# Expert weights in 1 MB transfers: the gate/up slots of a mixture-of-experts loop filled and given back by halves

## The chip, the cores and the metric

One NeuronCore of a Trainium2 chip runs the whole kernel. The metric is the device time of one execution in microseconds (us). The kernel before took 1300.48 us, the median of three executions (1299.77 to 1305.3). The profile is of one further execution, which took 1301.27 us; its traced span, from the first to the last instruction, is 1299.4 us.

## The reference, cut to what matters

One decoder layer over 256 tokens of width 1024, all in float32: three attention-like branches are merged into the residual stream, and then a mixture of experts adds its share. Only the second part matters here. Each token picks 4 of 32 experts; an expert is a product with a 1024 x 2048 matrix (gate and up columns interleaved), a clamped SwiGLU, and a product with a 1024 x 1024 matrix.

```python
def expert_block(args):
    rows, wts, e = args
    hgu = tok[rows] @ w_gu[e] + b_gu[e]
    gate = jnp.minimum(hgu[:, 0::2], SWIGLU_LIMIT)
    up = jnp.clip(hgu[:, 1::2], -SWIGLU_LIMIT, SWIGLU_LIMIT)
    act = (up + 1.0) * (gate * jax.nn.sigmoid(SWIGLU_ALPHA * gate))
    y = act @ w_down[e] + b_down[e]
    return y.astype(jnp.float32) * wts[:, None]
```

The weights of the 32 experts are 32 x 12 MB, and each is read from HBM once. They are the largest part of the 455.63 MB that the kernel moves.

## The kernel before, in words

**Trunk.** Up to about 375 us the three branches run, with their weights in a ring of six 2 MB slots. At the end of this stretch the router's choice is turned into a list of items. An item is one expert with up to 32 of its tokens; this input gives 46 items, and a popular expert has several, which stand one behind the other. Two items make a pair.

**Slots.** One expert's weights are six chunks of 2 MB: chunks 0 to 3 are gate/up weights (`w_gu`), chunks 4 and 5 are down weights (`w_down`). In SBUF there are twelve slots of 2 MB, six for experts on even seats and six for those on odd seats (`slot_no`). Chunk q of `w_gu` holds the weight rows 8p + 2q and 8p + 2q + 1 on partition p, which lie one behind the other in HBM, 16 KB in all. A chunk of `w_down` holds on each partition two stretches of 8 KB that lie apart in HBM. Each slot has a semaphore `w_full`, which the transfer raises by 16 when all of it has landed.

**SyncE (SP)** issues every weight transfer, in one fixed order. Experts 0 and 1 are loaded while the trunk runs (`load_chunk` called directly). In the loop, `load_round` serves one expert after the other: it waits until TensorE has used chunk q of the expert's last item (L505, `gu_done`), and then loads chunk q of the expert after the next into that slot (L394). Behind chunk 1 it waits for `brow_used` (L508) and loads the four 2 KB pieces of the gate/up bias row (L510). Chunks 4 and 5 follow, behind waits for `down_done` (L513). All of this stands in one instruction stream, so that a wait holds up everything behind it. There are 30 such rounds.

**TensorE (PE)** runs over the pairs. `up(q, ...)` (L1094) waits in `landed` (L1083) for the whole chunk q and multiplies it by the tokens, as 2 halves c = 0, 1 of four products each (each recorded as two matmuls, so 16 for a chunk), and its last matmul raises `gu_done` by one. `up(0)` waits for the bias row too. `bias` is L1073, `down` L1119, the gather of tokens L1045, the scatter of results L1053, the turning of activations L1104. The order for one pair is: gather, the first item's chunk 0 and bias, the down product of the item before, the first item's chunks 1 to 3, scatter, the second item's chunk 0 and bias, the first item's down product, the second item's chunks 1 to 3.

**VectorE (DVE)** waits for the item's fourth `gu_done` (L1850) and applies the clamps (L1853 and after). ScalarE (ACT) applies the sigmoid and evacuates the results (L1410 to L1423).

Of the kernel before, what the change touches and what calls it, by code (L numbers as in the profile page):

```python
# [30 lines left out]
P = 128  # L31
# [160 lines left out]
def hybrid_layer(nc, A, const, out):  # L192

    with ExitStack() as ctx:
# [5 lines left out]
        def S(name):  # L200
            if name not in sems:
                sems[name] = ctx.enter_context(nc.semaphore(name))
            return sems[name]
# [19 lines left out]
        slot = [mem[:, a:a + SLOT] for a in slots_at]  # L223
# [18 lines left out]
        w_full = [S(f"w_full{i}") for i in range(NSLOTS)]  # L242

        def C(name):
            a, n = CPART[name]
            return late[:, a:a + n] if a < LATE else cst[:, a - LATE:a - LATE + n]
# [132 lines left out]
        w_gu, b_gu, w_dn = A["w_gu"][0], A["b_gu"][0], A["w_down"][0]  # L379
# [3 lines left out]
        def slot_no(q, odd):  # L383

            return q if not odd else NSLOT + q if q < 4 else 6 + q

        def load_chunk(sp, e, q, odd):

            if q < 4:
                n, src = 2, w_gu[e].rearrange("(p c) n -> p c n", p=P)[:, 2 * q:2 * q + 2, :]  # L390
            else:
                n, src = 2, w_dn[e].rearrange("(c p two) n -> p c (two n)", p=P, two=2)[:, 2 * (q - 4):2 * (q - 4) + 2, :]
            n_slot = slot_no(q, odd)
            sp.dma_start(slot[n_slot].rearrange("p (c n) -> p c n", c=n), src).then_inc(w_full[n_slot], 16)  # L394


        def lines(a):
# [14 lines left out]
        def _(sp):  # L412
            for i in range(NT):
                sp.dma_start(memn[:, i, :], A["mem"][0][P * i:P * i + P, :]).then_inc(mem_in[i], 16)
            def cols(a, c0, n=512):
                return a[:, c0:c0 + n].rearrange("(c p) n -> p c n", p=P)

            src = {
                "mk": cols(w_mkv, 0), "mv": cols(w_mkv, 512), "mq": cols(w_in, C_MQ),
                "qk0": cols(w_in, 0), "qk1": cols(w_in, 512), "v": cols(w_in, C_V), "o": cols(w_in, C_O),  # L420
                "nq": cols(w_in, C_NQ), "nkv": cols(w_in, C_NKV), "kcvc": cols(w_in, C_KCVC, 256),
                "w1k": A["cmp_w1_k"][0].rearrange("(m l) d f -> (l d) m f", l=2),
                "w1v": A["cmp_w1_v"][0].rearrange("(m l) d f -> (l d) m f", l=2),
                "wbm": cols(A["w_br_mem"][0], 0, D), "wbl": cols(A["w_br_ml"][0], 0, D),
                "wbn": cols(A["w_br_nsa"][0], 0, D),
                "wo0": cols(A["w_out"][0], 0), "wo1": cols(A["w_out"][0], 512),
# [73 lines left out]
            def load_round(n, odd):  # L500

                f = sp.value_load(idx[0:1, bass.ds(n, 1)], min_val=0, max_val=ITEMS - 1)
                ahead = sp.value_load(idx[0:1, bass.ds(n + (AT_ORDER + 1), 1)], min_val=0, max_val=NE - 1)
                for q in range(4):
                    sp.wait_ge(S("gu_done"), f * 4 + (q + 1))  # L505
                    load_chunk(sp, ahead, q, not odd)
                    if q == 1:
                        sp.wait_ge(S("brow_used"), f + 1)  # L508
                        for m in range(4):
                            sp.dma_start(brow[not odd][32 * m:32 * m + 1, :],  # L510
                                         b_gu[bass.ds(ahead, 1), 512 * m:512 * m + 512]).then_inc(brow_in[not odd], 16)
                for q in (4, 5):
                    sp.wait_ge(S("down_done"), f * 2 + (q - 3))  # L513
                    load_chunk(sp, ahead, q, not odd)
# [41 lines left out]
        def _(pe):  # L556
# [50 lines left out]
            for half in range(2):  # L607
# [6 lines left out]
                for k in range(4 * half, 4 * half + 4):  # L614
                    for i in range(NT):
                        mm = nc.tensor.matmul(both[i][:, :], memT[:, k, P * i:P * i + P], w[:, k, :],
                                              start=k == 0, stop=k == KT - 1)
# [15 lines left out]
            for n in range(4):  # L633
                w = slot3(f"qk{n // 2}", KT, 512)
                b = begin(f"qk{n}")
                for j in range(2):
                    c0 = 256 * (n % 2) + P * j
                    for k in range(KT):
                        mm = nc.tensor.matmul(b[:, 256 * j:256 * j + 256], w[:, k, c0:c0 + P], uT[:, k, :],  # L639
                                              start=k == 0, stop=k == KT - 1)  # L640
# [7 lines left out]
            for k in range(KT):  # L648
                g = k % 4
                mm = nc.tensor.matmul(b[32 * g:32 * g + 32, 0:SEQ], wgw[:, k, :], uT[:, k, :], start=k < 4, stop=k >= 4)  # L650
# [6 lines left out]
            for j in range(2):  # L657
                mm = nc.tensor.matmul(b[0:4, 256 * j:256 * j + 256], C("sum4")[:, 4 * j:4 * j + 4], gws, start=True, stop=True)
# [39 lines left out]
            for i in range(NT):  # L698
                mm = nc.tensor.matmul(b[:, 24 * i:24 * i + 24], gws[:, P * i:P * i + P], C("sum4")[:, 8:32], start=True, stop=True)
# [57 lines left out]
            for j in range(2):  # L757
                for k in range(KT):
                    mm = nc.tensor.matmul(b[:, 256 * j:256 * j + 256], w[:, k, P * j:P * j + P], uT[:, k, :],
                                          start=k == 0, stop=k == KT - 1)  # L760
# [7 lines left out]
            for n, (name, job) in enumerate((("w1k", "hk"), ("w1v", "hv"))):  # L768
# [4 lines left out]
                for m in range(4):  # L773
                    for g in range(4):
                        mm = nc.tensor.matmul(b[32 * g:32 * g + 32, 0:CMP_HID], blk[:, n, 4 * m + g, :],
                                              w[:, 4 * m + g, :], start=m == 0, stop=m == 3)
                done(mm, job)
            bgate("bgl", 0, 0)
            for n, job in enumerate(("hk", "hv")):
                was_read(pe, job)  # L780
                b = begin(job + "T")
                for f in range(2):
                    mm = nc.tensor.matmul(b[:, 32 * f:32 * f + 32], hidp[:, n, P * f:P * f + P], C("sum4"), start=True, stop=True)
# [9 lines left out]
            for f in range(2):  # L793
                mm = nc.tensor.matmul(b[0:30, 0:DH], hid[:, 0, f, :], w2[:, 0, f, :], start=f == 0, stop=f == 1)
# [3 lines left out]
            for g in range(2):  # L798
                for f in range(2):
                    mm = nc.tensor.matmul(b[0:NCMP, DH * g:DH * g + DH], hid[:, 1, f, NCMP * g:NCMP * g + NCMP],  # L800
                                          w2[:, 1, f, :], start=f == 0, stop=f == 1)
# [104 lines left out]
            for hh in range(2):  # L906
                for j in range(2):
                    job = f"pn{hh}{j}"
                    b = begin(job)
                    for u in range(2):  # L910
                        c0 = 512 * hh + 256 * j + P * u
                        for k in range(4):
                            was_read(pe, f"nv{k}")
                            mm = nc.tensor.matmul(b[:, 256 * u:256 * u + 256], w[:, k, c0:c0 + P], hT_nsa[k],  # L914
                                                  start=k == 0, stop=k == 3)
# [28 lines left out]
            for k in range(KT):  # L944
# [3 lines left out]
                mm = nc.tensor.matmul(b[32 * g:32 * g + 32, 0:SEQ], wr[:, k, :], uT[:, k, :], start=k < 4, stop=k >= 4)  # L948
# [3 lines left out]
            for i in range(NT):  # L952
                mm = nc.tensor.matmul(b[:, NE * i:NE * i + NE], lTs[:, P * i:P * i + P], C("sum4"), start=True, stop=True)
# [33 lines left out]
            for i in range(NT):  # L987
                mm = nc.tensor.matmul(b[0:NE, 33:34], sel[:, i, :], ones[:, 0:1], start=i == 0, stop=i == NT - 1)
# [30 lines left out]
            mm = nc.tensor.matmul(b[0:1, 3 * ITEMS:3 * ITEMS + NE], C("pcol")[0:NE, :], Hs, start=True, stop=True)  # L1019
# [57 lines left out]
            def trunk_turns(n_slot):  # L1077
                return TRUNK_TURNS[n_slot] if n_slot < NSLOT else 0

            def landed(q, e, odd):  # L1080

                n_slot = slot_no(q, odd)
                pe.wait_ge(w_full[n_slot], e * 8 + (8 if odd else 16 * (trunk_turns(n_slot) + 1)))  # L1083
                return slot[n_slot]

            def up(q, e, n, odd):

                if q == 0:
                    pe.wait_ge(brow_in[odd], e * 32 + (32 if odd else 64))
                w = landed(q, e, odd).rearrange("p (c n) -> p c n", c=2)  # L1090
                for c in range(2):
                    k = 2 * q + c
                    for s in range(4):
                        mm = nc.tensor.matmul(BH[n][32 * s:32 * s + 32, :], xgT[:, k, 32 * n:32 * n + 32],  # L1094
                                              w[:, c, 512 * s:512 * s + 512], start=k == 0, stop=k == KT - 1,
                                              skip_group_check=True)
                mm.then_inc(S("gu_done"), 1)

            def turn(i, n, j):

# [347 lines left out]
        def _(dve):  # L1448
# [79 lines left out]
            for n in range(2):  # L1528
                dve.wait_ge(S("conv_sig"), n + 1)
                q = qk[:, 4 * n:4 * n + 4, :].rearrange("p j t -> p (j t)")  # L1530
# [55 lines left out]
            for i in range(NT):  # L1586
                was_read(dve, f"nq{i}")
                q = nq_sb[:, i, :].rearrange("p (h e) -> p h e", h=QH)
# [47 lines left out]
            for n in range(2):  # L1636
                for g in range(2):
                    src = k2[:, n, g, :]
                    src = bass.AP(src.tensor, src.offset, [list(src.ap[0]), [2, 16], [16, NCMP]])
# [207 lines left out]
            step(V.tensor_copy(idx[0:1, AT_PACK:AT_PACK + PAIRS], packed), "idx_ready")  # L1847
            def activate(i, n):

                dve.wait_ge(S("gu_done"), i * 4 + 4)  # L1850
                h = BH[n][:, :].rearrange("p (f two) -> p f two", two=2)
                g, u = gt, ut
                V.tensor_scalar(g, h[:, :, 0], LIMIT, None, ALU.min).then_inc(S("g_clip"), 1)  # L1853
                V.tensor_scalar(u, h[:, :, 1], -LIMIT, LIMIT, ALU.max, ALU.min).then_inc(S("u_clip"), 1)
                dve.wait_ge(S("g_sig"), i + 1)
                V.tensor_tensor(g, g, sg, ALU.mult).then_inc(S("gs_done"), 1)
                dve.wait_ge(S("u_clip"), i + 1)
                dve.wait_ge(S("gs_done"), i + 1)
                V.scalar_tensor_tensor(out=u, in0=u, scalar=1.0, in1=g, op0=ALU.add, op1=ALU.mult).then_inc(S("act_ready"), 1)
# [52 lines left out]
```

## Time and profile before

| What | Value |
|---|---|
| Median of three executions | 1300.48 us |
| The profiled execution | 1301.27 us |
| Its span | 1299.4 us |
| PE busy | 1119.9 us (86%) |
| DVE, ACT busy | 269.4 us, 217.2 us |
| Data moved | 455.63 MB, mean 351 GB/s |

Busy times are summed over the span and say little of what sets the end: they are averages over a trunk and a loop with different limits. The page cuts the span into 40 slices of 32.5 us with a busy digit for each engine (9 is 90% or more), and beneath them the share of time in which the 16 DMA engines were busy and the GB/s that they moved. A DMA share can come out slightly above 1, since the records of packets overlap. "SPq" is SyncE's sequencer, which issues transfers and is never counted as busy.

### The profile page before, as it was taken

What the parts mean: (1) busy time and instruction counts of PE and PEld (TensorE: products, weight loads), DVE (VectorE), ACT (ScalarE), POOL (GpSimd) and SP (SyncE); (2) the same over time, 40 slices, a digit from 0 to 9 for tenths busy, and PEclk for the clock granted to TensorE, in tenths of its full rate; (3) what the DMA queues carried; (4) which work ended last, traced back from release to release, by engine and by line L of the source; (5) the groups of instructions that cost most, each with busy time, mean ns of one, the idle gap of its engine ahead of it and who ended that gap; (6) DMA issues with size and microseconds to landing.
All of it is one profiled execution on the core that took longest, in us unless ns stands there. A gap on an engine that the chain in (4) does not pass through costs nothing.

```text
span 1299.4 us, 19302 instructions
## 1 busy us (share of the span) xinstructions
PE 1119.9 (86%) x7511; PEld 536.1 (41%) x7512; DVE 269.4 (21%) x728; ACT 217.2 (17%) x486; POOL 17.4 (1%) x24
## 2 busy tenths in 40 slices
PE   8999999999999996569976965899597969799957
PEld 4665767888553332123322321333222323243312
DVE  3234424363231111001111100011111101111101
ACT  2115422254021110001100100111010101011101
POOL 1100101000000000000000000000000000000000
PEclk9999999999999998779987977899888979899978
DMA  9942237343679999999999999979999999999996
GB/s 335 356 136 91 91 131 270 123 167 138 262 294 422 423 427 425 427 425 425 426 425 429 425 427 426 426 294 428 426 427 427 424 425 425 428 427 427 425 425 263
DMA packets 66886, 455.63 MB, mean 351 GB/s; under 512 B 7588, under 2 KB 13576, under 8 KB 34088
## 3 DMA queue, kind: packets, MB, share of 16 engines
q1 hardware_dynamic: 66344, 454.48, 85.3%
q10 hardware_dynamic: 448, 0.60, 0.1%
q8 instruction: 21, 0.34, 0.1%
q0 software_dynamic: 64, 0.13, 0.0%
q14 instruction: 9, 0.07, 0.0%
HBM read 454.15 MB, written 1.05 MB: 350 GB/s over the span
## 4 chain that ended last, share of the span: by engine, by line
PE 66%; DMA 23%; SPq 8%; issue 1%; DVE 1%; ACT 1%; ACTq 0%; DVEq 0%
DMA mq<-in_b_gu 22%; PE bank L1094 18%; PE bank L1119 10%; PE bank L590 6%; PE bank L730 6%; SPq L394 4%; PE bank L1045 4%; PE bank L1053 3%; PE bank L1073 3%; SPq L510 3%; PE bank L639 2%; PE bank L926 2%; PE bank L892 2%; PE bank L579 1%; PE bank L914 1%
## 5 line engine op out<-in xcount | busy, mean ns | idle before, releaser
L1094 PE MATMUL bank<-mem 128*32 128x512 f32 x2944 | 359.2, 630 | 156.7 <-DMA mq<-in_b_gu 156.4
L1094 PEld LDWEIGHTS bank<-mem 128*32 128x32 f32 x2944 | 94.7, 114 | 366.9 <-issue 364.2
L1119 PE MATMUL bank<-mem 128*32 128x512 f32 x1472 | 173.0, 611 | 0.7 <-ACT mem L1415 0.7
L1853 DVE TENSOR_SCALAR mem<-bank 128x256 f32<-128x256 f32 x46 | 19.5, 424 | 742.6 <-PE bank L1094 742.6
L1421 ACT ACTIVATE mq<-bank 64x512 f32<-64x512 f32 x46 | 27.1, 590 | 463.0 <-PE bank L1119 463.0
L1119 PEld LDWEIGHTS bank<-mem 128*32 128x32 f32 x1472 | 44.2, 112 | 129.4 <-issue 128.7
L1045 PEld LDWEIGHTS bank<-mem,sc 128*128 128x128 f32 x736 | 83.9, 192 | 19.2 <-issue 19.2
L1045 PE MATMUL bank<-mem,sc 128*128 128x64 f32 x736 | 87.1, 277 | 0.0
L590 PE MATMUL bank<-mem 128*128 128x512 f32 x192 | 83.2, 592 | 0.0
L1053 PE MATMUL bank<-mq,mem 128*128 128x512 f32 x176 | 81.4, 605 | 0.0
L730 PE MATMUL bank<-mem 128*128 128x256 f32 x320 | 71.3, 381 | 0.0
L730 PEld LDWEIGHTS bank<-mem 128*128 128x128 f32 x320 | 60.0, 190 | 8.7 <-issue 0.7
L590 PEld LDWEIGHTS bank<-mem 128*128 128x128 f32 x192 | 36.3, 190 | 43.6 <-issue 43.5
L1410 ACT ACTIVATE mem<-mem 128x256 f32<-128x256 f32 x46 | 19.2, 417 | 208.6 <-DVE mem L1853 208.6
L1073 PE MATMUL bank<-mq,mem 1*32 1x512 f32 x368 | 52.7, 644 | 0.0
L1053 PEld LDWEIGHTS bank<-mq,mem 128*128 128x128 f32 x176 | 31.6, 189 | 50.0 <-issue 50.0
L1415 ACT ACTIVATE mem<-bank 128x256 f32<-128x256 f32 x46 | 17.6, 383 | 141.2 <-PE bank L1108 74.4
L892 PE MATMUL bank<-mem 128*128 128x256 f32 x128 | 28.7, 380 | 0.0
L1073 PEld LDWEIGHTS bank<-mq,mem 1*32 1x32 f32 x368 | 7.4, 109 | 50.3 <-issue 50.3
L579 PE MATMUL bank<-mem 128*128 128x128 f32 (+4 forms) x150 | 20.3, 275 | 8.7 <-DMA mem<-shape_consts 5.8
L926 PE MATMUL bank<-mem 128*128 128x512 f32 x64 | 27.8, 592 | 0.0
L639 PE MATMUL bank<-mem 128*128 128x256 f32 x128 | 27.8, 379 | 0.0
(306 smaller groups left out, 794.5 us busy)
## 6 DMA issues: line engine op xcount, KB each, us to landing
mem<-in_w_gu SPq DMA_DIRECT2D x128, 2048.0 KB, 32.7
mem<-in_w_down SPq DMA_DIRECT2D x64, 2048.0 KB, 37.1
mem<-in_w_in SPq DMA_DIRECT2D x13, 2048.0 KB, 10.5
mem<-in_w_out SPq DMA_DIRECT2D x2, 2048.0 KB, 8.4
mem<-in_w_mem_kv SPq DMA_DIRECT2D x2, 1024.0 KB, 7.1
mem<-in_w_mem_kv SPq DMA_DIRECT2D x1, 2048.0 KB, 8.3
mem<-in_cmp_w_k SPq DMA_DIRECT2D x1, 2048.0 KB, 8.5
mem<-in_cmp_w_v SPq DMA_DIRECT2D x1, 2048.0 KB, 8.1
```

Source lines behind the costliest of these rows:

```text
L394: sp.dma_start(slot[n_slot].rearrange("p (c n) -> p c n", c=n), src).then_inc(w_full[n_slot], 16)
L510: sp.dma_start(brow[not odd][32 * m:32 * m + 1, :], b_gu[bass.ds(ahead, 1), 512 * m:512 * m + 512]).then_inc(brow_in[not odd], 16)
L590: mm = nc.tensor.matmul(b[:, 0:n], src[k][:, P * i:P * i + P], w[:, k, c0:c0 + n], start=k == 0, stop=k == kt - 1)
L639: mm = nc.tensor.matmul(b[:, 256 * j:256 * j + 256], w[:, k, c0:c0 + P], uT[:, k, :], start=k == 0, stop=k == KT - 1)
L730: mm = nc.tensor.matmul(b[:, 256 * j:256 * j + 256], w[:, k, c0 + P * j:c0 + P * j + P], src[k], start=k == 0, stop=k == kt - 1)
L892: mm = nc.tensor.matmul(b[:, 256 * half:256 * half + 256], w[:, k, c0:c0 + P], uT[:, k, :], start=k == 0, stop=k == KT - 1)
L926: mm = nc.tensor.matmul(b[:, :], mg[k][:, P * i:P * i + P], w[:, k, :], start=k == 0, stop=k == KT - 1)
L1045: mm = nc.tensor.matmul(b[:, 64 * c:64 * c + 64], x2[:, t, o:o + P], Gm[:, t].rearrange("p g n -> p (g n)"), start=t == 0, stop=t == NT - 1)
L1053: mm = nc.tensor.matmul(ACC[t][hh][:, :], STs[:, P * t:P * t + P], y_sb[:, 512 * hh:512 * hh + 512], start=False, stop=False, skip_group_c ...
L1073: mm = nc.tensor.matmul(BH[n][p:p + 32, :], ones[p:p + 1, 0:32], brow[row][p:p + 1, :], start=False, stop=False, skip_group_check=True)
L1094: mm = nc.tensor.matmul(BH[n][32 * s:32 * s + 32, :], xgT[:, k, 32 * n:32 * n + 32], w[:, c, 512 * s:512 * s + 512], start=k == 0, stop=k ...
L1119: mm = nc.tensor.matmul(BG[64 * hh + 32 * two:64 * hh + 32 * two + 32, :], actT[:, o:o + 32], w[:, 2 * c + two, 512 * hh:512 * hh + 512], ...
```

## The change

Three things are altered together. `load_chunk` fetches a gate/up chunk by two transfers of 1 MB instead of one of 2 MB: half c is the weight row 8p + 2q + c of each partition, 8 KB. In the loop each half has a wait of its own. TensorE raises `gu_done` after each half of a chunk rather than after the chunk, so that all counts of `gu_done` double (SP's, and VectorE's L1850), and the count of `w_full` for a gate/up slot goes up by 32 for each chunk. TensorE still waits for both halves before it starts a chunk. The down chunks keep their single 2 MB transfers.

```diff
-        def load_chunk(sp, e, q, odd):
+        def load_chunk(sp, e, q, odd, halves=range(2)):
+            n_slot = slot_no(q, odd)
             if q < 4:
-                n, src = 2, w_gu[e].rearrange("(p c) n -> p c n", p=P)[:, 2 * q:2 * q + 2, :]
+                src = w_gu[e].rearrange("(p c) n -> p c n", p=P)
+                for c in halves:
+                    sp.dma_start(slot[n_slot][:, 2048 * c:2048 * c + 2048].unsqueeze(1),
+                                 src[:, 2 * q + c:2 * q + c + 1, :]).then_inc(w_full[n_slot], 16)
             else:
-                n, src = 2, w_dn[e].rearrange("(c p two) n -> p c (two n)", p=P, two=2)[:, 2 * (q - 4):2 * (q - 4) + 2, :]
-            n_slot = slot_no(q, odd)
-            sp.dma_start(slot[n_slot].rearrange("p (c n) -> p c n", c=n), src).then_inc(w_full[n_slot], 16)
+                src = w_dn[e].rearrange("(c p two) n -> p c (two n)", p=P, two=2)[:, 2 * (q - 4):2 * (q - 4) + 2, :]
+                sp.dma_start(slot[n_slot].rearrange("p (c n) -> p c n", c=2), src).then_inc(w_full[n_slot], 16)
...
                 for q in range(4):
-                    sp.wait_ge(S("gu_done"), f * 4 + (q + 1))
-                    load_chunk(sp, ahead, q, not odd)
+                    for c in range(2):
+                        sp.wait_ge(S("gu_done"), f * 8 + (2 * q + c + 1))
+                        load_chunk(sp, ahead, q, not odd, (c,))
...
-                pe.wait_ge(w_full[n_slot], e * 8 + (8 if odd else 16 * (trunk_turns(n_slot) + 1)))
+                n = 32 if q < 4 else 16
+                pe.wait_ge(w_full[n_slot], e * (n // 2) + (n // 2 if odd else 16 * trunk_turns(n_slot) + n))
...
-                mm.then_inc(S("gu_done"), 1)
+                    mm.then_inc(S("gu_done"), 1)
...
-                dve.wait_ge(S("gu_done"), i * 4 + 4)
+                dve.wait_ge(S("gu_done"), i * 8 + 8)
```

## Rows read from the trace of the kernel before

**Rows 1.** The page's slices: PE busy tenths, DMA busy tenths, GB/s, packet counts.

```profile
PE   8999999999999996569976965899597969799957
DMA  9942237343679999999999999979999999999996
GB/s 335 356 136 91 91 131 270 123 167 138 262 294 422 423 427 425 427 425 425 426 425 429 425 427 426 426 294 428 426 427 427 424 425 425 428 427 427 425 425 263
DMA packets 66886, 455.63 MB, mean 351 GB/s; under 512 B 7588, under 2 KB 13576, under 8 KB 34088
```

**Rows 2.** Who waited for whom: engine line <- releaser: us, times, longest.

```profile
PE bank L1094 <- DMA mq<-in_b_gu: 156.4, 14, 13.5
```

**Rows 3.** The chain that ended last: start us, us, what; two items' period repeats.

```profile
668.36 28.89 DMA mq<-in_b_gu
...
728.15 28.87 DMA mq<-in_b_gu
...
787.93 28.88 DMA mq<-in_b_gu
```

**Rows 4.** Timeline of PE, 816 to 882 us: start us, us, instructions merged.

```profile
816.93 3.64 PE L1094 MATMUL bank<-mem 128*32 128x512 f32 x16 [12.75 <-DMA mq<-in_b_gu]
...
865.89 1.93 PE L1094 MATMUL bank<-mem 128*32 128x512 f32 x16
867.74 1.06 PE L1073 MATMUL bank<-mq,mem 1*32 1x512 f32 x8
868.74 3.64 PE L1119 MATMUL bank<-mem 128*32 128x512 f32 x32
872.19 5.33 PE L1094 MATMUL bank<-mem 128*32 128x512 f32 x48
877.46 3.70 PE L1053 MATMUL bank<-mq,mem 128*128 128x512 f32 x8
```

**Rows 5.** Timeline of SP's issues, same columns, from 823 us on.

```profile
823.89 6.63 SPq L394 DMA_DIRECT2D mem<-in_w_down  x2
868.02 6.62 SPq L394 DMA_DIRECT2D mem<-in_w_gu  x2
874.89 1.53 SPq L510 DMA_DIRECT2D mq<-in_b_gu  x4
876.66 1.42 SPq L394 DMA_DIRECT2D mem<-in_w_gu  x2
886.28 2.10 SPq L394 DMA_DIRECT2D mem<-in_w_down  x2
890.17 0.95 SPq L394 DMA_DIRECT2D mem<-in_w_gu  x2
```

**Rows 6.** Stretches: us, engines' busy (instructions), PE clock, DMA share, GB/s.

```profile
25.00:30.00 5.00, 5.00 (x16) 2.40 (x15) 3.62 (x9) 0.32 (x1) 1.02 (x1) 1.00 1.05 398
35.00:40.00 5.00, 5.00 (x13) 2.19 (x12) 0.00 (x0) 0.69 (x1) 0.00 (x0) 1.00 1.05 387
55.00:60.00 5.00, 5.00 (x25) 4.41 (x24) 2.52 (x6) 0.04 (x1) 2.32 (x3) 1.00 1.05 387
860.00:865.00 5.00, 5.00 (x50) 3.58 (x38) 2.03 (x5) 0.42 (x1) 0.00 (x0) 1.00 0.22 90
865.00:870.00 5.00, 5.00 (x45) 1.71 (x47) 0.62 (x2) 0.66 (x2) 0.00 (x0) 1.00 0.33 51
870.00:875.00 5.00, 5.00 (x52) 1.56 (x48) 0.00 (x0) 1.18 (x2) 0.00 (x0) 1.00 0.90 367
```

**Rows 7.** Page's transfers: count, KB each, median us from issue to landing.

```profile
mem<-in_w_gu SPq DMA_DIRECT2D x128, 2048.0 KB, 32.7
mem<-in_w_down SPq DMA_DIRECT2D x64, 2048.0 KB, 37.1
mem<-in_w_in SPq DMA_DIRECT2D x13, 2048.0 KB, 10.5
```

**Rows 8.** Line L394's own instructions on SP: count, ns min/median/max, first and last start.

```profile
L394 SPq FUSED_REGOPS  x180: 37/37/43, 385.5 to 1249.1; - x180
```

## The prediction, made before the changed kernel ran

> **What bounds the kernel now.** I read the 40 slices first. From slice 13 to slice 39 the DMA engines are busy nine tenths or more, but for one slice, and move 422 to 429 GB/s, while PE's digit falls to 5 to 7 again and again [rows 1]. Next the waits: PE stood still before L1094 for 156.4 us in 14 waits, at most 13.5 us, all ended by a transfer landing [rows 2]. In the chain that ended last, such a landing returns with an even beat: 668.36, 728.15, 787.93, so 59.8 us for two experts or 24 MB [rows 3]. Issue to landing takes 32.7 us in the median for gate/up [rows 7], while the twelve chunks of two experts take 59.8 us, 4.98 each: the queue is 32.7 / 4.98, over six chunks, deep. So in the loop the DMA engines set the pace, and PE has some 12 us to spare in most pairs. What the change does is worth what it does to those engines: to their idle time, and to their time per byte.
>
> Idle time of the DMA engines in the loop is found in one place. The slice at 294 GB/s holds it, and narrower stretches show 90 GB/s in 860 to 865, 51 in 865 to 870 and 367 in 870 to 875 [rows 1, 6]. There PE works without a break from 816.93 on items of one popular expert; SP has issued all it may by about 830.5 (823.89 + 6.63), and the next slot comes free only when chunk 0 is used by that expert's last item, at 865.89 + 1.93; SP issues at 868.02 [rows 4, 5].
>
> **The parts of the change.**
>
> Finer release, the gain. In the drained stretch the first 1 MB can be asked for after 8 of the 16 matmuls of 1.93 us, so 0.9 us earlier [rows 4]. Behind it, chunk 1's release comes some 6.2 us after chunk 0's (two issues begin and end within 868.02 + 6.62, and the last takes under 0.5) [rows 5], while a 2 MB chunk needs 4.98 us of the engines; here too the first half may go 0.9 us earlier, which fills a small second bubble. The engines' restart moves by the 0.9 us; both bubbles together could give at most 2 x 0.9 = 1.8 us. I take -0.9. Everywhere else the queue holds chunks enough that asking earlier only means waiting longer in it: nothing.
>
> PE's landing wait still wants both halves, so nothing starts earlier on the far side of the transfer. The end of the kernel hangs on down chunks, which are not split.
>
> Smaller packets, the cost. The page counts 66886 packets, 34088 of them under 8 KB [rows 1]. The difference, 32798, is 128 x 128 (one packet of 16 KB on each partition for each gate/up chunk) plus 64 x 256 (two of 8 KB for each down chunk), which is 32768, plus 30 others. So gate/up goes in 16 KB packets now, and the halves make them 8 KB: on each of the 16 engines a gate/up chunk becomes 16 packets instead of 8.
>
> What does a packet cost beyond its bytes? Two rows fix it. In the trunk the engines are full with 2 KB packets (w_in, 512 columns of float32): 387 GB/s in two stretches and 398 in a third [rows 6]. At 387, a 2 KB packet takes one engine 16 x 2048 / 387e3 = 0.0847 us. Call y the time of 2 KB and k the cost per packet: y + k = 0.0847. In the loop, an engine moves in 59.785 us (the mean beat) 24 MB / 16 = 768 times 2 KB in 64 + 64 = 128 packets, and the engine that carries the bias rows (one packet each, 8 in two experts) has 8 packets of 2 KB more: 768 y + 128 k + 8 (y + k) = 59.785 [rows 3]. This gives 640 y = 48.27, y = 0.0754 us, k = 9.3 ns. At 398 GB/s instead it gives y + k = 0.0823 and k = 6.4 ns. I take 9.3, which two of the three stretches give.
>
> Eight further packets cost a gate/up chunk 8 x 9.3 = 74 ns (51 ns at the low end). The loop loads 30 x 4 = 120 of these chunks. Some lie between the landing that lets PE go at 816.93 and the drained stretch, whose end PE sets; they only shorten the idle time. In those 49 us (to 866) the engines move 49 / 4.98 = 10 chunks, of which two thirds, 6, are gate/up. 114 x 0.074 = +8.5 us; low end 114 x 0.051 = +5.9. The eight chunks loaded in the trunk are fetched one or two at a time as slots come free, beside PE's trunk work; were all of them on the path, it would be 8 x 0.074 = 0.6 us. I take nothing.
>
> One more completion for each chunk on each engine. The trace doesn't price it apart. From below it is nothing (a gain is excluded: work is only added); from above one small packet, k, as the nearest row: 114 x 9.3 ns = 1.1 us. In the beat above the 8 bias transfers fit without a price for their completions; I take the middle, +0.5.
>
> SP: per round four more waits, each with one register operation of 37 ns [rows 8], and four more issues. Two issues end 0.95 us after the first began [rows 5], about 0.5 us each; I take 0.6 with the wait around it: 4 x 0.6 = 2.4 us in a round of 29.9 us. Queued behind them are the bias rows, the down chunks and the next round; the depth of the DMA queue hides it. In the drained stretch that cover is gone, but there the two halves come free 0.9 us apart, longer than the 0.6 us of an issue. Without any cover it would be 30 x 2.4 = 72 us, which the depth excludes. An issue that finds the queue full holds SP up already (6.63 us for two [rows 5]); that costs nothing as long as the queue is what is full.
>
> PE: one more increment per chunk and item, 184 in all. Three chunks run in one piece, 872.19 to 877.46, 0.110 us a matmul with two increments inside; one chunk takes 1.85 for 16, 0.116 [rows 4]. No cost is seen, and there are 12 us of slack per pair. DVE's wait only has another number.
>
> **Sum**: -0.9 + 8.5 + 0.5 = +8.1 us. The profiled span should go from 1299.4 to 1307.5 and its execution from 1301.27 to 1309.4; against the median of the runs shown, 1300.48 + 8.1 = 1308.6 us. The bounds of this case are 5.9 + 0 - 1.8 = +4.1 and 8.5 + 1.1 = +9.6 with no gain at all: 1304.6 to 1310.1.
>
> **What the Trainium skill says of it.** The page "DMA: Bandwidth & Descriptors", section "Bandwidth" (its part on why small descriptors are slow), gives a fixed overhead of about 3 cycles for each packet, and the same section an 850 MHz fabric; that would be 3.5 ns instead of 9.3, by estimate 114 x 8 x 3.5 ns = 3.2 us instead of 8.5. By that rule the sum would be +2.8 us, 1303.3. The same page's fit charges each transfer a fixed 2 us beside its bytes, which would add 2 us for each of the 120 further transfers; it would give a 2 MB chunk 6.8 us where the trace has 4.98 in a deep queue, so the fixed part is hidden here, and I don't count it.
>
> **Rivals.**
>
> Not slower: a packet costs next to nothing, and the lower rate in the trunk belongs to w_in's narrow columns, not to packets. Then the change is the -0.9 us of the drained stretch and the time 1299.6; if a packet costs about a third of my figure it is 114 x 8 x 3.1 ns = 2.8, less 0.9, +1.9: 1302.4. It decides from k below (6.5 + 0.9 - 0.5) / (114 x 8) = 7.6 ns on: there the slowdown falls under 0.5%. For it: the trunk stretches are short and 398 GB/s is among them. Against it: with k = 0 the beat gives y = 59.785 / 776 = 0.0770 us, and 2 KB packets would then run at 16 x 2048 / 77.0 = 425 GB/s; the trunk shows 387 to 398 with the engines full. The 3 cycles of the Trainium skill's page "DMA: Bandwidth & Descriptors", section "Bandwidth", would end near this case's upper value.
>
> Much slower: a cost per transfer, not per packet. If all of the 128 x 9.3 = 1190 ns that I lay on packets in two experts belonged to their 12 large transfers, each would cost 99 ns, and the change adds 114 of them: +11.3 - 0.9 = +10.4, 1310.9. If both exist, 8.5 + 11.3 - 0.9 = +18.9, 1319.4. The same range stands for 8 KB pieces at a 64 KB stride being read less well than the down chunks' 8 KB pieces, which lie close together. Against it: w_in's transfers are of 2 MB as well [rows 7] and yet run slower.
>
> Faster by over 6.5 us: the drained stretch would have to go altogether. The missing bytes there, (425 - 90 + 425 - 51 + 425 - 367) x 5 us, are 3.8 MB or 9 us of the full rate, but no half is free before 0.9 us ahead of today's release.
>
> **How the numbers follow.** The forecast case, a cost per packet of 6.4 to 9.3 ns, 0.64; little or no cost per packet (1299.6 to 1302.4), 0.18; cost per transfer or a worse stride (1310.9 to 1319.4), 0.15; faster, 0.03. The range 1302.0 to 1313.0 takes in the forecast's bounds, the upper end of the second case and the lower part of the third. A measurement of this kernel can tell about 0.5%, 6.5 us, from no change, so above 1307.0 counts as slower: the third case and, of the first, the part near 9.3 ns, some 0.46 of its 0.64. Slower 0.61, within 0.5% 0.36, faster 0.03.
>
> **What the profile of the changed kernel would show.** 66886 + 16384 packets, and with them 128 x 16 = 2048 tiny completions, so about 85,300, of which some 36,100 under 8 KB. The beat of two experts at 59.79 + 8 x 0.074 = 60.4 us, and the full slices at 420 to 423 GB/s instead of 425 to 427. The issue after the drained stretch 0.9 us earlier after PE's chunk began than today's 2.1 us. If the queue counts packets, issue to landing falls for gate/up from 32.7 us to some 20 to 25, at no cost; that would not be a sign of speed. I am wrong if the beat stays at 59.8 (no packet cost), if it exceeds 60.8 (a cost per transfer), or if the DMA share shows new dips, which would mean that the shorter queue runs dry.

## The result and the profile after

The changed kernel takes 1309.26 us in the median of 14 runs (1305.63 to 1311.44), the kernel before 1300.25 us in 14 (1298.87 to 1308.0). The ratio is 1.0059 with a 95% interval of 1.0044 to 1.0073, so it is slower by 5.7 to 9.5 us. The profiled execution of the changed kernel has a span of 1306.9 us, 7.5 more than before.

The page's slices of the changed kernel, as in [rows 1]:

```profile
DMA  9932337334589999999999999979999999999995
GB/s 339 348 134 92 115 134 266 126 138 173 225 335 419 420 421 423 422 422 422 422 421 422 422 422 421 422 319 423 422 421 422 422 422 422 422 421 422 422 422 242
DMA packets 85319, 455.64 MB, mean 349 GB/s; under 512 B 9636, under 2 KB 15624, under 8 KB 36136
```

The same bytes go in 18433 packets more: 16384 data packets and 2048 completions, with one over. The full slices stand at 419 to 423 GB/s, where they stood at 422 to 429. DMA is as busy as before; it is busy for longer with each byte. The drained slice (the 27th) has 319 GB/s instead of 294.

The chain that ended last, changed kernel (start us, us, what), against [rows 3]:

```profile
983.13 21.39 DMA mq<-in_b_gu
...
1043.53 21.40 DMA mq<-in_b_gu
...
1103.91 21.38 DMA mq<-in_b_gu
```

(1103.91 - 983.13) / 2 = 60.39 us for two experts. Before it was 59.785. That is the whole change in one line: +0.60 us for every 24 MB. The waits of PE for a landing are as they were [rows 2]:

```profile
PE bank L1099 <- DMA mq<-in_b_gu: 157.7, 14, 13.3
```

And the page's transfers, against [rows 7] (KB each, median us from issue to landing):

```profile
mem<-in_w_gu SPq DMA_DIRECT2D x256, 1024.0 KB, 24.7
mem<-in_w_down SPq DMA_DIRECT2D x64, 2048.0 KB, 27.9
```

From issue to landing a transfer now takes 8 to 9 us less, and the kernel is slower. For gate/up a part of this is only that a transfer is half as large: in the first run below, with 2 MB transfers of 8 KB packets, it is 29.0 us. A down transfer is as large as before and takes 27.9 us instead of 37.1. So an issue-to-landing time in a full queue does not tell the speed; it tells how much is queued ahead.

The drained stretch, changed kernel: first PE, then SP's issues, then the stretches in which the engines run dry, as in [rows 4 to 6].

```profile
819.54 3.64 PE L1099 MATMUL bank<-mem 128*32 128x512 f32 x16 [12.93 <-DMA mq<-in_b_gu]
...
868.50 1.92 PE L1099 MATMUL bank<-mem 128*32 128x512 f32 x16
```

```profile
869.76 7.46 SPq L393 DMA_DIRECT2D mem<-in_w_gu  x4
877.47 1.54 SPq L514 DMA_DIRECT2D mq<-in_b_gu  x4
879.25 2.45 SPq L393 DMA_DIRECT2D mem<-in_w_gu  x4
```

```profile
865.00:870.00 5.00, 5.00 (x48) 3.74 (x47) 2.08 (x6) 0.96 (x3) 0.00 (x0) 1.00 0.05 21
870.00:875.00 5.00, 5.00 (x48) 1.35 (x48) 0.00 (x0) 0.00 (x0) 0.00 (x0) 1.00 0.85 316
```

SP asks for the first half 869.76 - 868.50 = 1.26 us after TensorE begins that chunk; before, the whole chunk was asked for after 868.02 - 865.89 = 2.13 us. The finer release works, by 0.87 us, in the one place of the loop where the engines wait for it.

### The profile page after: what moved, and what is told of

It is laid out like the page before. It is cut to its first block, busy times and chain, and to the rows that moved or that the text cites. A ratio compares the mean times of both kernels' runs of the same rounds, so it can differ in the third digit from the quotient of the medians.

```text
span 1306.9 us, 19790 instructions
## 1 busy us (share of the span) xinstructions
PE 1126.2 (86%) x7511; PEld 536.1 (41%) x7512; DVE 269.7 (21%) x728; ACT 217.0 (17%) x486; POOL 17.4 (1%) x24
## 4 chain that ended last, share of the span: by engine, by line
PE 60%; SPq 20%; DMA 15%; issue 3%; DVE 1%; ACT 1%; ACTq 0%; DVEq 0%
PE bank L1099 15%; DMA mq<-in_b_gu 15%; SPq L393 11%; PE bank L1124 8%; PE bank L594 6%; PE bank L734 6%; SPq L397 5%; SPq L514 4%; PE bank L1057 3%; PE bank L1049 3%; PE bank L1077 3%; PE bank L643 2%; PE bank L930 2%; PE bank L896 2%; PE bank L583 1%
## 5 line engine op out<-in xcount | busy, mean ns | idle before, releaser
L1099 PE MATMUL bank<-mem 128*32 128x512 f32 x2944 | 359.2, 630 | 158.4 <-DMA mq<-in_b_gu 157.7
## 6 DMA issues: line engine op xcount, KB each, us to landing
mem<-in_w_gu SPq DMA_DIRECT2D x256, 1024.0 KB, 24.7
mem<-in_w_down SPq DMA_DIRECT2D x64, 2048.0 KB, 27.9
```

## The experiments

Three explanations of the 0.60 us a beat were on the table: a cost for each packet (the prediction's), a cost for each transfer, and a cost of the added waits and increments. The first four runs take them apart; the last three turn to what else loads the DMA engines. "Beat" is the time of two experts in the steady part of the loop, read from the chain as above.

**The packets alone.** One transfer of 2 MB and one release, but of two rows that lie apart in HBM.

```diff
-                n, src = 2, w_gu[e].rearrange("(p c) n -> p c n", p=P)[:, 2 * q:2 * q + 2, :]
+                n, src = 2, w_gu[e].rearrange("(p c q) n -> p c q n", p=P, q=4)[:, :, q, :]
```

(The gathered tokens and the gains are put in the matching order: an access pattern of x2 at L1401 and of gcol at L1865.)

> A gate/up chunk stays one transfer of 2 MB with one wait and one release, but holds the weight rows 8p + q and 8p + q + 4, which lie apart in HBM, so its packets are of 8 KB as in the changed kernel. Theory (a cost for each packet, 9.3 ns): the beat of two experts goes from 59.79 to 60.4 us as in the changed kernel, some 83,300 packets, and the time to about 1309 us, +9 against before, without the 0.9 us that the halves win. Rival 1 (a cost for each transfer): the number of transfers is unchanged, so beat 59.8 and 1300 us. Rival 2 (the waits and issues added on SyncE cost): none is added here, so 1300 us too.

Measured: 1312.09 us, ratio 1.0088 (1.0072 to 1.0105); span 1307.8. Its packets and the chain that ended last:

```profile
DMA packets 83270, 455.63 MB, mean 348 GB/s; under 512 B 7588, under 2 KB 13576, under 8 KB 34088
```

```profile
678.72 22.01 DMA mq<-in_b_gu
...
799.46 22.01 DMA mq<-in_b_gu
```

Four experts in 120.74 us, 60.37 a beat. No transfer, wait or increment was added, and the whole slowdown is there. The median is 3 us above the 1309 expected, and the interval of the ratio, +9.4 to +13.7 us, begins a little above +9; why this kernel is slower than its beat asks for is open. The profile is of one of its faster executions (1309.79 us); its span, 1307.8, is 0.9 above that of the changed kernel, the size of the release that this kernel lacks, but one profile each can't show that this is the reason. This run leaves one rival: its packets, too, are read at a stride of 64 KB. The fourth run has no such stride.

**The halves without the finer release.**

```diff
-                    for c in range(2):
-                        sp.wait_ge(S("gu_done"), f * 8 + (2 * q + c + 1))
-                        load_chunk(sp, ahead, q, not odd, (c,))
+                    sp.wait_ge(S("gu_done"), f * 4 + (q + 1))
+                    load_chunk(sp, ahead, q, not odd)
...
-                    mm.then_inc(S("gu_done"), 1)
+                mm.then_inc(S("gu_done"), 1)
...
-                dve.wait_ge(S("gu_done"), i * 8 + 8)
+                dve.wait_ge(S("gu_done"), i * 4 + 4)
```

> The changed kernel with its two transfers of 1 MB for a gate/up chunk, but both issued behind one wait for the whole chunk, and gu_done raised once for a chunk as before. Theory: beat 60.4 us as in the changed kernel, and the issue after the drained stretch comes some 2.1 us after TensorE's chunk began, as before, rather than 1.26 us: 1310 us, 0.9 more than the changed kernel. Rival (the release in halves is what costs, by the waits on SyncE or the increments on TensorE): beat back at 59.8, 1300 to 1302 us.

Measured: 1309.82 us, ratio 1.0074 (1.0058 to 1.009); span 1306.7. The chain, then PE around the drained stretch:

```profile
557.09 21.38 DMA mq<-in_b_gu
...
798.65 21.40 DMA mq<-in_b_gu
```

```profile
820.18 3.54 PE L1098 MATMUL bank<-mem 128*32 128x512 f32 x16 [13.34 <-DMA mq<-in_b_gu]
...
868.76 1.92 PE L1098 MATMUL bank<-mem 128*32 128x512 f32 x16
...
945.41 1.08 PE L1098 MATMUL bank<-mem 128*32 128x512 f32 x4 [14.19 <-DMA mq<-in_b_gu]
```

The changed kernel at the same place:

```profile
944.24 2.79 PE L1099 MATMUL bank<-mem 128*32 128x512 f32 x12 [13.28 <-DMA mq<-in_b_gu]
```

SP in this run:

```profile
870.89 7.12 SPq L393 DMA_DIRECT2D mem<-in_w_gu  x4
```

Eight experts in 241.56 us, 60.39 a beat, as in the changed kernel: waits and increments cost nothing there. The first issue comes 870.89 - 868.76 = 2.13 us after the chunk's start, as before the change. From one wait's end to the next across the drained stretch this kernel takes 945.41 - 820.18 = 125.23 us, the changed one 944.24 - 819.54 = 124.70: the release in halves is worth 0.5 us there, in one profile of each. Against the changed kernel the two medians differ by 0.6 us, which these runs can't tell from nothing.

**The transfers alone.** The down chunks, in 8 KB packets already, each by two transfers.

```diff
-            sp.dma_start(slot[n_slot].rearrange("p (c n) -> p c n", c=n), src).then_inc(w_full[n_slot], 16)
+            dst = slot[n_slot].rearrange("p (c n) -> p c n", c=n)
+            for c in (range(0, 2) if q >= 4 else ()):
+                sp.dma_start(dst[:, c:c + 1, :], src[:, c:c + 1, :]).then_inc(w_full[n_slot], 16)
+            if q < 4:
+                sp.dma_start(dst, src).then_inc(w_full[n_slot], 16)
```

(L1083's count of `w_full` is altered to match.)

> The kernel before with its down chunks, which go in 8 KB packets already, fetched by two transfers of 1 MB instead of one of 2 MB: 64 more transfers, not one more data packet. Theory (a cost for each packet): four more completions in a beat, each between 0 and 9.3 ns, so the beat is 59.79 to 59.83 us and the time within 1 us of before. Rival (99 ns for each transfer): beat 59.79 + 4 x 0.099 = 60.2 us, time +5.7 us, 1306.

Measured: 1299.36 us, ratio 0.9997 (0.9985 to 1.0008); span 1297.5.

```profile
667.65 28.24 DMA mq<-in_b_gu
...
727.41 28.29 DMA mq<-in_b_gu
...
787.19 28.25 DMA mq<-in_b_gu
```

59.77 us a beat, where before has 59.785. Four more transfers in a beat, and with them four more completions on each engine, cost nothing that the trace can show. The rival of 99 ns a transfer would be 0.4 us a beat and is out. The +0.5 us that the prediction set aside for completions (over 114 chunks, 4.4 ns each) would be 4 x 4.4 ns = 0.02 us a beat here; nothing of it is seen, but this is about as fine as a beat can be read.

**The packets at another place.** Down chunks in 4 KB packets, gate/up untouched.

```diff
-                n, src = 2, w_dn[e].rearrange("(c p two) n -> p c (two n)", p=P, two=2)[:, 2 * (q - 4):2 * (q - 4) + 2, :]
+                n, src = 4, w_dn[e].rearrange("(c p) n -> p c n", p=P)[:, 4 * (q - 4):4 * (q - 4) + 4, :]
...
-                    a = ut.rearrange("p (f two) -> p f two", two=2)[:, :, two]
+                    a = ut[:, P * two:P * two + P]
```

> The kernel before with each down chunk's rows spread so that a 2 MB transfer is made of 4 KB packets, 32 for each DMA engine instead of 16; gate/up untouched, the number of transfers unchanged. Theory: 64 more packets on each engine in a beat, as many as the change adds, so 59.79 + 64 x 0.0093 = 60.4 us and about 1309 us, the same loss as the change's by another road. Rivals (a cost for each transfer, or a gate/up read whose 64 KB stride is slow): beat 59.8 and 1300 us.

Measured: 1307.28 us, ratio 1.0048 (1.0035 to 1.0062).

```profile
560.25 20.34 DMA mq<-in_b_gu
...
801.75 20.33 DMA mq<-in_b_gu
```

Eight experts in 241.50 us, 60.38 a beat: 64 more packets for each engine, +0.59 us, in another tensor, from 8 to 4 KB rather than from 16 to 8. So the cost is 0.59 / 64 = 9.2 ns for a packet, the same at both steps, and neither the 64 KB stride of the halves nor the gate/up weights have a part in it. The median lies 1.7 us below the 1309 expected, and the interval of the ratio, +4.5 to +8.1 us, ends a little short of +9. The profile is of the slowest of the five executions, 1312.74 us; the other four lie between 1307.12 and 1307.98.

The packet records in the traces agree in kind. In the loop a packet of 16 KB is recorded with 615 ns in the mean, one of 8 KB with 314, one of 4 KB with 164: two packets take 13 ns longer than one of twice the size, at both steps. The records of packets overlap a little, so that not all of the 13 ns counts; the beat says that 9.2 do.

**What the last engine does.** The prediction's equation let one engine carry the bias pieces and set the beat. One transfer of four pieces instead:

```diff
-                        for m in range(4):
-                            sp.dma_start(brow[not odd][32 * m:32 * m + 1, :],
-                                         b_gu[bass.ds(ahead, 1), 512 * m:512 * m + 512]).then_inc(brow_in[not odd], 16)
+                        sp.dma_start(brow[not odd][0:P:32, :],
+                                     b_gu[bass.ds(ahead, 1), :].rearrange("e (m n) -> (e m) n", m=4)).then_inc(brow_in[not odd], 16)
```

(The loads ahead of the loop and L1089's count are altered to match.)

> The kernel before with the bias row of an expert fetched by one transfer of four pieces (4 partitions x 2 KB) instead of four transfers of one piece each; weights untouched. Theory: the four single pieces all went through the same DMA engine, which does 0.35 us more than the others in each round, and since a chunk counts as landed when its last engine is done, that engine sets the beat. One transfer of four pieces spreads them over more engines, one each, at 0.09 us. In the kernel before the last engine fell 0.21 us a round behind the last but one, so the beat should fall by 2 x (0.13 to 0.21) to between 59.37 and 59.53 us, and the time by 3.7 to 6.0 us, to 1294.5 to 1297. Rival (the 16 engines share the load evenly, so that only the sum of packets counts): 59.79 and 1300 us.

Measured: 1294.49 us, ratio 0.9959 (0.9946 to 0.9972); span 1291.0.

```profile
657.88 35.36 DMA mq<-in_b_gu
...
776.39 35.34 DMA mq<-in_b_gu
...
902.13 33.29 DMA mq<-in_b_gu
```

Here the ends count, since the pieces differ in length: (811.73 - 693.24) / 2 = 59.25 us a beat, 0.5 less than before, and 5.8 us in the median, for the same bytes in the same packets. The beat is 0.1 us below the expected range here, and 59.36 us behind the drained stretch. The run with the down chunks in halves speaks against the number of transfers as the reason, though its transfers were large ones.

The traces show the engine itself. In the kernel before, the four bias packets follow one another, 84 ns long and 86 ns apart, as they would on one engine (606.33, 606.41, 606.50, 606.58 us); with one transfer they overlap (632.89 and 632.91). Each of the 16 engines reports the end of its share of a chunk. For one slot, in four landings running from 631.8 to 811.2 us, the last report of the kernel before came 0.91, 1.65, 2.31 and 2.76 us behind the last but one; with one transfer it was 0.26, 0.27, 0.23 and 0.16. So from about 600 us on one engine fell further and further behind the others, and its work paced the loop, not the sum over 16. Up to about 570 us no engine stood out so (0.07 us between the last two at 512.79), and that slot landed with a beat of 59.04 us (453.75 to 512.79); behind the drained stretch the two are level again, 0.02 us apart, and the lag grows anew.

**The change turned round.** Down chunks in 16 KB packets.

```diff
-                n, src = 2, w_dn[e].rearrange("(c p two) n -> p c (two n)", p=P, two=2)[:, 2 * (q - 4):2 * (q - 4) + 2, :]
+                n, src = 1, w_dn[e].rearrange("(d p r) n -> p d (r n)", p=P, r=4)[:, q - 4:q - 3, :]
...
-                                              w[:, c, 512 * s:512 * s + 512], start=k == 0, stop=k == KT - 1,
+                                              w[:, c, 1024 * (s // 2):1024 * (s // 2) + 1024].rearrange(
+                                                  "p (m b j) -> p m b j", b=2, j=4)[:, :, s % 2, :], start=k == 0, stop=k == KT - 1,
```

(The bias row, in two pieces of 4 KB by one transfer, is read in the same order.)

> The change turned round, on the kernel before: gate/up stays in 16 KB packets and the down chunks get them too, 8 packets of 16 KB for each engine instead of 16 of 8 KB. For this TensorE reads the gate/up weights' columns in pieces of 4 out of 8, and the bias row goes in one transfer as two pieces of 4 KB. Theory (9.3 ns for each packet): 64 packets fewer in a beat, -0.59 us, and the bias on two engines at some 0.16 us a round instead of 0.35 on one, another -0.2 to -0.38: beat 58.8 to 59.0, time 1300.3 - 8.5 - (3 to 5) = 1287 to 1289 us. Rival (TensorE reads pieces of 16 bytes more slowly): the mean of the gate/up matmuls rises above 630 ns and TensorE, with 12 us to spare in a pair, uses that up; above some 850 ns the kernel gets slower than before.

Measured: 1295.08 us, ratio 0.9963 (0.995 to 0.9976), well short of the 1287 to 1289 expected.

```profile
L1094 PE MATMUL bank<-mem 128*32 128x512 f32 x2944 | 358.1, 629 | 150.0 <-DMA mq<-in_b_gu 149.7
```

```profile
650.06 43.79 DMA mq<-in_b_gu
...
768.40 43.81 DMA mq<-in_b_gu
```

TensorE reads the pieces at the old pace, 629 ns. The beat, by the ends, is (812.21 - 693.85) / 2 = 59.18 us, not 58.8 to 59.0. This miss was in my own count: two down chunks a round lose 8 packets each, which makes 32 in a beat and not 64. With 32 the expected beat is 59.1 to 59.3, and 4 of the 6 to 8 us by which the time missed are accounted for. The rest shows in a last run.

**Both at once**, with the right count: down in 16 KB packets, the bias row on four engines. The transposed activations are laid out for it by small products.

```diff
-                for two in range(2):
-                    a = ut.rearrange("p (f two) -> p f two", two=2)[:, :, two]
-                    mm = nc.tensor.transpose(BX[:, P * two:P * two + P], a, ident)
+                a = ut.rearrange("p (f r) -> p f r", r=4)
+                unit = ident.rearrange("p (d b t) -> p d b t", d=2, b=2)
+                for r in range(4):
+                    for b in range(2):
+                        mm = nc.tensor.matmul(BX[64 * b:64 * b + 64, 64 * r:64 * r + 64], a[:, :, r], unit[:, :, b, :],
+                                              start=True, stop=True)
```

> Down chunks in 16 KB packets together with the bias row on four DMA engines. The down matmuls take the hidden units in another order (unit 512 d + 4 p + r on partition p), made by eight small products with the unit matrix in the place of two turns, so that TensorE reads all weights in whole rows and the bias row keeps its four 2 KB pieces in one transfer. A correction to what was expected of down_16k: two down chunks in a round with 8 packets fewer each make 16 a round and 32 a beat, not 64, so 0.30 us a beat and not 0.59. Theory with the right count: the beat of bias_one (59.36 us) less 32 x 0.0093 = 59.06 us, the time 1294.5 less 28.5 x 0.15 = 1290.2 us. Rival (the down chunks' packets don't matter, and down_16k owed all of its gain to the bias row): 59.36 us and 1294.5.

Measured: 1294.88 us, ratio 0.9967 (0.9954 to 0.9979); span 1292.5.

```profile
658.10 35.97 DMA mq<-in_b_gu
...
768.48 43.77 DMA mq<-in_b_gu
...
907.45 31.19 DMA mq<-in_b_gu
...
1086.17 29.63 DMA mq<-in_b_gu
```

With only the bias row altered:

```profile
1080.19 33.30 DMA mq<-in_b_gu
```

The expected beat was worked out from the 59.36 us that the run with the bias row has behind the drained stretch. There it comes true: (1115.80 - 938.64) / 3 = 59.05 against (1113.49 - 935.42) / 3 = 59.36, so 0.31 us for 32 packets where 9.2 ns each make 0.29. Ahead of the drained stretch the beat is (812.25 - 694.07) / 2 = 59.09 us against 59.25, only 0.16 less. The time is not what was expected. Between the wait that ends at 812.25 and the next in this list, at 938.64, lie 126.4 us; with the bias row alone altered the same stretch is 935.42 - 811.73 = 123.7. It holds the popular expert, and there TensorE sets the pace. PE from that wait to the release that ends it, first this kernel, then the one with only the bias row altered:

```profile
812.37 3.64 PE L1092 MATMUL bank<-mem 128*32 128x512 f32 x16 [8.69 <-DMA mq<-in_b_gu]
...
829.41 1.18 PE L1104 MATMUL bank<-mem 128*64 128x64 f32 x16
...
863.93 1.92 PE L1092 MATMUL bank<-mem 128*32 128x512 f32 x16
```

```profile
811.86 3.48 PE L1092 MATMUL bank<-mem 128*32 128x512 f32 x16 [9.89 <-DMA mq<-in_b_gu]
...
828.60 0.44 PE L1102 MATMUL bank<-mem 128*128 128x128 f32 x2
...
860.38 1.92 PE L1092 MATMUL bank<-mem 128*32 128x512 f32 x16
```

863.93 - 812.37 = 51.56 us against 48.52. The eight small products take 1.18 us where two turns took 0.44, and three such turns are 2.3 of the 3.0 us. DMA time was saved in the loop and paid back where DMA isn't the limit. The longer stretch, 126.4 against 123.7, is 2.7 of the 4.7 us by which the median missed the 1290.2 expected; the smaller gain ahead of it may be another part, and the rest is open. In the run with 16 KB packets and plain turns this stretch took 50.99 us, 2.5 more than 48.52, for another reason: after the long wait TensorE ran at half clock for longer. Its down product there, and the stretches around it (us, busy, clock, DMA share, GB/s):

```profile
817.76 5.08 PE L1120 MATMUL bank<-mem 128*32 128x512 f32 x32
```

```profile
815.00:818.00 3.00, 3.00 (x20) 0.40 (x16) 0.00 (x0) 0.00 (x0) 0.00 (x0) 0.50 1.01 431
818.00:821.00 3.00, 3.00 (x20) 0.64 (x16) 0.00 (x0) 0.00 (x0) 0.00 (x0) 0.55 1.03 437
```

5.08 us at a granted clock of 0.50 to 0.55, near the lower level of 1.2 GHz, for what takes 3.64 in the others. Why the clock came back later in this profile is open. The length of the wait alone doesn't decide it: TensorE had stood still for 12.26 us here, and in the kernel before for 12.75 us, after which the same down product took 3.64. The version to keep is the kernel before with the bias row in one transfer, 1294.49 us: faster than both kernels, and nothing tried on top of it was faster still (1294.88 and 1295.08).

## Why the prediction was right, point by point

**What bounds the loop.** Right. PE's waits for landings stayed (157.7 us after, 156.4 before), and in every kernel the beat followed the load of the DMA engines; the run with the bias row narrows this to the load of the fullest one.

**The cost of a packet.** Right in mechanism and size. It was put at 9.3 ns out of a trunk stretch of 2 KB packets and the loop's beat; two kernels that alter nothing but packets (the first, in gate/up; the fourth, in down) give (60.37 - 59.785) / 64 = 9.1 and 9.2 ns. The predicted beat was 60.4 us, the measured one 60.39. The choice of 387 GB/s over 398 decided between +8.1 and +5.5 and was the right one; it rested on two stretches against one, and so was in part luck. That one engine carries the bias rows and sets the beat was a term of the equation, and the landings bear it out from about 600 us on. (The low end, 114 x 0.051, is 5.8 and not 5.9.)

The rule of the Trainium skill, page "DMA: Bandwidth & Descriptors", section "Bandwidth", with about 3 cycles for a packet, would come to 3.5 ns by an estimate with its 850 MHz. The runs have 9.2 ns at 4, 8 and 16 KB; the measurement decides. The fixed 2 us stand in the same page's section "Anatomy of one DMA — SWDGE (gpsimd) path", in a fit for transfers that GpSimd issues; here SyncE issues them into a full queue, and they did not show at all: four more transfers in a beat left it at 59.77 us.

**One more completion.** Mis-sized: taken at +0.5 us out of 0 to 1.1; the run with four more for each engine in a beat shows none of it (59.77 against 59.785 us).

**The finer release.** -0.9 us was taken. The first issue did move by 0.87 us. Across the whole drained stretch the gain against the same kernel without it is 0.5 us in one profile each.

**SP, PE, DVE.** Right, they cost nothing: with or without the waits and increments the beat is 60.39 us.

**The shorter queue.** Issue to landing was put at 20 to 25 us for gate/up and came to 24.7; no new dip in the DMA share. That the queue counts packets was only supposed, and no run here tests it alone.

**The sum.** +8.1 us was predicted, +7.5 measured in the spans, +9.0 in the medians, and +5.7 to +9.5 by the ratio. The span holds something that the sum doesn't have. The first issue of the loop comes at 383.89 us rather than 385.67; 0.9 of this is the half chunk, the rest lies in the trunk, where in the profile before TensorE fell to a lower clock for a moment and in the profile after it didn't. The stretch before and after:

```profile
116.00:122.00 6.00, 4.36 (x15) 3.66 (x16) 3.07 (x8) 3.12 (x9) 0.00 (x0) 0.72 0.97 316
```

```profile
116.00:122.00 6.00, 4.02 (x20) 3.07 (x20) 3.44 (x8) 4.15 (x12) 0.00 (x0) 1.00 1.03 332
```

In both kernels PE stood still for some 2 us just ahead of it. From the first issue to the end the loop took 1306.9 - 383.89 = 923.0 us against 913.7; 9.3 more, of which 0.9 because the first issue is half a chunk early. That leaves +8.4 for the sum's +8.1. In part the close match is luck: the +0.5 for completions was not there, and two runs of the same packet cost have medians of 1312.09 and 1307.28 us.

**The rivals.** "A packet costs next to nothing" fell with the first and the fourth run, "a cost per transfer" with the first and the third, and a worse stride with the fourth. Slower by over 0.5% had a chance of 0.61; the ratio, 1.0059, lies above that bound, but its interval begins at 1.0044, so the kernel is surely slower and not surely by that much.

## What to carry to other kernels

When the DMA engines are full, count packets for each engine and not transfers: splitting a transfer cost nothing here, but splitting it so that each partition's contiguous run got shorter cost each engine some 9 ns for every further packet, 1.5% of a 4.98 us chunk at 8 KB instead of 16. A finer release only pays where the queue runs dry; find these stretches first (here one, of some 9 us, and it gave back 0.5 to 0.9). And look at what single pieces go to which engine, since a chunk has landed when its last engine is done.

## What was not expected of the hardware

A few tiny transfers were worth nearly two thirds of the whole change. The four 2 KB bias pieces of a round, 8 KB beside 12 MB, cost 30 rounds some 0.2 us each, 5.8 us in all, because they queued on one engine and the others' lead was of no use. Which engine it is, the traces don't name.

The granted clock of TensorE differed between kernels in stretches whose instructions are the same (0.72 and 1.00 in the trunk, 0.50 to 0.55 and 1.00 behind a long wait). By this a single profile's span can be off by 1 to 2 us (0.9 in the trunk, some 2.3 behind the long wait), which is why the beat was the better measure for effects of half a microsecond.
